# A hybrid decoder layer on eight cores: two x tiles of the third token group loaded from another point and into other slots, and another planned order

## What is computed

```python
h = rmsnorm(x, norm_mix_pre)
q, k, v, u = split(h @ w_in)                 # 512 channels each
q, k = rope(q), rope(k)                      # 8 heads of 64
y_attn = moba_attention(q, k, v)             # each query: own 256-key block (causal)
                                             # and its top 3 earlier blocks by q . mean(k)
y_pool = pool_mixer(u, w_pool, b_pool, pool_scale)   # trailing means over 2/4/8/16 tokens
x = x + rmsnorm(concat(y_attn, y_pool) @ w_out, norm_mix_post)
h = rmsnorm(x, norm_ffn_pre)
f = (silu(conv3(h @ w_gate)) * conv3(h @ w_val)) @ w_down    # 2816 channels each
out = x + rmsnorm(f, norm_ffn_post)
```

## Time and profile before

| | |
|---|---|
| median of 3 runs | 779.73 us (776.73 to 795.33) |
| the profiled execution | 778.17 us |
| its span, slowest core (core 7) | 776.6 us |
| spans of the eight cores | 768.8 to 776.6 us |
| TensorE busy on core 7 | 754.9 us, 97% |
| VectorE, ScalarE, GpSimd busy | 60%, 50%, 37% |

### The profile page before, as it was taken

One profiled execution on the slowest core, in us unless ns is written; L12 is line 12 of the kernel. 1 busy time (PEld: TensorE's weight loads), 2 busy tenths in 40 slices (PEclk: granted clock), 3 DMA queues, 4 the chain that ended last, 5 costly groups with the idle time before them and its releaser, 6 DMA issues.

```text
span 776.6 us, 14872 instructions; the slowest of 8 cores (768.8 to 776.6 us)
## 1 busy us (share of the span) xinstructions
PE 754.9 (97%) x4866; PEld 385.0 (50%) x4866; DVE 469.2 (60%) x702; ACT 387.4 (50%) x619; POOL 286.7 (37%) x309
## 2 busy tenths in 40 slices
PE   7997999999999999999999999999999999999996
PEld 5644655455655555444444444444444444444443
DVE  4786658654555555578787781322877877772223
ACT  3835567158899999554554440211445454441111
POOL 1273324301455560557655562100343444321000
PEclk9899899999999999999999999999999999999998
DMA  8978589119579565678897676342444444001321
GB/s 256 321 243 199 81 187 198 50 28 144 108 193 215 161 170 131 109 136 160 169 194 122 116 115 102 106 166 108 109 82 82 69 71 79 1 0 57 110 99 62
DMA packets 63067, 99.21 MB, mean 128 GB/s; under 512 B 35856, under 2 KB 41872, under 8 KB 61968
## 3 DMA queue, kind: packets, MB, share of 16 engines
q1 hardware_dynamic: 50304, 65.88, 31.2%
q0 software_dynamic: 12688, 32.38, 25.6%
HBM read 100.60 MB, written 16.78 MB: 151 GB/s over the span
## 4 chain that ended last, share of the span: by engine, by line
PE 90%; DMA 3%; DVE 2%; issue 2%; ACT 1%; POOL 1%; SPq 1%; DVEq 0%; ACTq 0%; POOLq 0%
PE ps L954 38%; PE ps L1072 18%; PE ps L830 7%; PE ps L904 7%; PE ps L769 7%; PE ps L674 5%; PE ps L848 4%; DMA MEM<-x 3%; PE ps L1065 1%; PE ps L835 1%; SPq L165 1%; PE ps L797 1%; ACT MEM L844 0%; PE ps L650 0%; DVE MEM L681 0%
## 5 line engine op out<-in xcount | busy, mean ns | idle before, releaser
L954 PE MATMUL ps<-MEM 128*128 128x512 bf16 x1408 | 309.8, 379 | 1.3 <-DVE MEM L975 1.3
L954 PEld LDWEIGHTS ps<-MEM 128*128 128x128 bf16 x1408 | 136.5, 98 | 164.0 <-issue 2.2
L965 ACT ACTIVATE MEM<-ps,MEM 128x1024 f32<-128x1024 f32 x88 | 105.9, 1203 | 147.2 <-PE ps L954 144.0
L844 ACT ACTIVATE MEM<-ps 128x512 bf16<-128x512 f32 (+1 forms) x320 | 149.4, 541 | 38.7 <-PE ps L835 17.1
L991 POOL TENSOR_TENSOR MEM<-MEM 128x1024 bf16<-128x1024 f32 x44 | 105.2, 2391 | 118.9 <-DVE MEM L978 82.0
L968 DVE SCALAR_TENSOR_TENSOR MEM<-ps,MEM 128x1023 f32<-128x1023 f32 x88 | 112.8, 1282 | 57.9 <-ACT MEM L965 57.7
L1072 PE MATMUL ps<-MEM 128*128 128x512 bf16 x660 | 142.8, 379 | 0.0
L971 DVE SCALAR_TENSOR_TENSOR MEM<-ps,MEM 128x1022 f32<-128x1022 f32 x88 | 112.7, 1281 | 8.2 <-DVE MEM L968 0.5
L1072 PEld LDWEIGHTS ps<-MEM 128*128 128x128 bf16 x660 | 64.4, 98 | 78.0
L830 PE MATMUL ps<-MEM 72*128 72x512 bf16 (+1 forms) x320 | 102.8, 349 | 0.1
L604 POOL TENSOR_SCALAR MEM<-MEM 128x1 f32<-128x1 f32 x63 | 13.7, 218 | 197.7 <-ACT MEM L1077 118.8
(11 more groups left out here) (103 smaller groups left out, 620.6 us busy)
## 6 DMA issues: line engine op xcount, KB each, us to landing
MEM<-w_up_r POOLq DMA_DIRECT2D x44, 512.0 KB, 5.5
MEM<-x SPq DMA_DIRECT2D x32, 512.0 KB, 5.5
x1s<-MEM SPq DMA_DIRECT2D x16, 512.0 KB, 5.4
MEM<-x1s SPq DMA_DIRECT2D x16, 512.0 KB, 3.9
out<-MEM SPq DMA_DIRECT2D x15, 512.0 KB, 2.6
MEM<-w_down POOLq DMA_DIRECT2D x22, 256.0 KB, 7.5
MEM<-w_qk SPq DMA_DIRECT2D x4, 1024.0 KB, 20.7
MEM<-MEM SPq DMA_DIRECT2D x24, 128.0 KB, 5.6
```

The source lines that it names most:

```text
L844: op("act", lambda e, c0=c0, u=u, p=p: e.activation(out=PT[p][:, c0:512], in_=bk[u.ids[0]][:, c0:512], func=AF.Exp, scale=SCALE), rd=u.b, ...
L954: mm = op("pe", lambda e, c=c, half=half, pr=pr, ws=ws, tb=tb: e.matmul(bk[pr.ids[tb]], lhsT=wu[ws][:, c, half * 128:(half + 1) * 128], rh ...
L965: op("act", lambda e, pr=pr, ch=ch, ts=ts: e.activation(out=tA[ts], in_=ps(pr)[:, :], func=AF.Identity, scale=cwb[:, ch, 2:3], bias=cwb[:, ...
```

## The change

Six edits. The planner's seed and the size of its jitter change (923 to 1348, 0.15 to 0.3), which reorders the streams. The plan counts 3 us more for the landing of every x load of `load_x`. Tiles 8 to 15 use slot (tt + 2) % 4: tile 8 in xs2, 9 in xs3, 10 in xs0, 11 in xs1. The loads of `next_x` follow that; those of the output projection (`sec1`) keep tt % 4. `bulk` no longer holds the landing of chunk 7, so a load of `next_x` waits for tile 7's landing and for its own slot alone. `scaled` takes the scaling of tile 1 instead of tile 3. All arithmetic, instructions and transfers stay.

```diff
-SEED, SHAKE = 923, 0.15
+SEED, SHAKE = 1348, 0.3
+X_LATE = 3.0
...
-    def dma(self, queue, key, pairs, ..., prio=None, turn=False):
+    def dma(self, queue, key, pairs, ..., prio=None, turn=False, late=0.0):
...
+            fin += o.get("late", 0.0)
             o["t0"], o["t1"] = t, fin
...
-        def load_x(tt, deps=()):
-            s = tt % 4
-            dma("sp", "fx%d" % s, [(xs[s], x_d[tt * 128:(tt + 1) * 128, :])], wr=[buf("xs%d" % s)], deps=deps)
+        def load_x(tt, deps=(), turn=0):
+            s = (tt + turn) % 4
+            dma("sp", "fx%d" % s, [(xs[s], x_d[tt * 128:(tt + 1) * 128, :])], wr=[buf("xs%d" % s)], deps=deps, late=X_LATE)
...
-            xsrc[tt] = (xs[tt % 4], buf("xs%d" % (tt % 4)))
+            xsrc[tt] = (xs[(tt + 2 * (tt > 7)) % 4], buf("xs%d" % ((tt + 2 * (tt > 7)) % 4)))
...
-            if tt == 3:
+            if tt == 1:
                 scaled.append(xb.w[-1])
...
-                load_x(tt, bulk if G < 3 else move1)
+                load_x(tt, bulk if G < 3 else move1, 2)
...
         lw = buf("ws%d" % wslot[7]).w[-1]
-        bulk.append(lw)
```

More of the change, by code:

```diff
@@ L159, in either, with dma @@
         return o
-    def dma(self, queue, key, pairs, rd=(), wr=(), wp=(), deps=(), nbytes=524288, cast=False, prio=None, turn=False):
+    def dma(self, queue, key, pairs, rd=(), wr=(), wp=(), deps=(), nbytes=524288, cast=False, prio=None, turn=False, late=0.0):
         raw = self._collect(queue, rd, wr, wp, deps)
@@ L165, in dma @@
         fn = lambda e: [e.dma_start_transpose(out=o_, in_=i_) if turn else e.dma_start(out=o_, in_=i_) for (o_, i_) in pairs]
-        o = dict(kind="dma", key=key, turn=turn, sig=False, seq=0, slack=0.0, ndma=len(pairs), nbytes=nbytes, cast=cast,
+        o = dict(kind="dma", key=key, turn=turn, sig=False, seq=0, slack=0.0, late=late, ndma=len(pairs), nbytes=nbytes, cast=cast,
                  alts={queue: (fn, (0.62 if queue == "pool" else 0.45) * len(pairs), 0.0)})
```

## The result

| | before | after |
|---|---|---|
| median | 778.78 us | 768.58 us |
| lowest to highest | 776.73 to 795.33 us | 768.33 to 768.68 us |
| span of the slowest core | 776.6 us | 767.1 us (core 1) |
| spans of the eight cores | 768.8 to 776.6 us | 765.8 to 767.1 us |

The changed kernel takes 0.987 of the time before, with a 95% interval of 0.985 to 0.990: 1.3% less, where 1.1% was forecast. In some runs, of every kernel alike, the cores of one die or of both show a lower clock and take longer (the 795.33 here); ratios leave such runs out. Its lines stand one or two further down than those of before (L620 is L622, L674 is L676, L769 is L771, L830 is L832, L848 is L850, L865 is L867).

A forecast was written before the change was run, and what follows sets the result against it. TensorE, busy 754.9 of 776.6 us, was taken as the bound, leaving idle time and low clock to win. 776.6 - 5.2 - 2.0 - 1.3 + 1.3 = 769.4 us of span, 771.0 us as execution time; range 766 to 778.

The forecast's parts named there:

- The stall, -5.2: TensorE's 5.9 us wait at line 848, behind late x loads of tiles 8 and 9, falls to 0.7; bounds 0 and -5.9.
- the clock behind it, -2.0: TensorE's low clock from 78 to 83 us, 2.0 us of work not done, goes if the wait at line 848 goes.
- The start, -1.3: Earlier V casts let 1.9 us of V matmuls fill TensorE's 2.7 us gap; seven tenths last; bounds 0 and -3.6.
- the 1.7 of the upper bound: Clock up from 20.6 to 24 us would win half of those 3.4 us, 1.7; counted at nothing.
- the lower bound's reason: Early V casts might win 0: later weights land no sooner, and TensorE could run dry for them.
- The new order, +1.3: Seed, jitter and 3 us more landing time reorder all streams; taken as 1.3 us lost, twice core 5's 0.7 rounded down.
- The bound of the order: Worst cost of reordering all streams: one more square placed too early, 5.9 + 2.0 us; other bound 0.
- The wait didn't move to the third tile: Rival: VectorE or ScalarE reaches tile 10's squares before its load lands or tile 8 is turned; 773 to 776 us; 0.17.
- the four operations only crowd the engines: Rival: two squares and two scalings, 4.4 us, delay exps and rope products from 60 to 70 us; 775 to 779; 0.08.
- SP held nothing: Rival: SP waits to turn tile 8 ahead of loading tiles 10 and 11; slower, 780 to 783 us; chance 0.07.
- More from the start: Rival: all 3.6 us won there, the stall quite gone, nothing lost to the order; 766.7 us; chance 0.10.
- The rule on packets: DMA engines alternate packets between queue rows, slowing group 0's last q copies; up to 2.7 us more, 772 to 774; 0.03.

The follow-up runs named there:

- the fixed ones: Kernel before with its stream order kept and only named operations moved; with early loads of tiles 8 and 9 alone 773.5 us, ratio 0.993.

## Why the prediction was right

**The stall, -5.2, and the clock behind it, -2.0.** Right: 5.3 of idle time and 2.0 of clock from 62 to 95 us. The early loads alone show the chain of the prediction, and the changed order with late loads shows that the loads are what removes the wait there. But the claim that this wait "goes" by the early load isn't general: the replanned kernel without them has no stall either. The landing of tiles 8 and 9 was forecast by about 59 and came at 56.3 and 59.5 on core 1 (up to 63.6 on core 6). Tiles 10 and 11 landed at 67.4 and 70.2, not at 71 to 73.

**The start, -1.3.** The sum's value holds (1.0 on the pair of cores above, 1.2 at the start of the attention with the casts alone, too little to be told in that kernel's time), but its working doesn't. The gap was to be filled by 1.9 us of matmuls, and the clock was counted at nothing. With the casts alone, busy time from 14 to 24 rose by 0.7 us over the eight cores and not at all on core 7, and most of what was won is clock (0.66 to 1.00 on core 7, 0.72 to 0.86 over the eight). This was the 1.7 of the upper bound, wrongly set to nothing. What takes some back is partly the lower bound's reason, weights that land no sooner: 0.48 us behind q/k weights on core 7 with the casts alone. In the changed kernel TensorE is idle 0.5 to 0.9 us of 24 to 31; on core 1 that wait is for a copy of turned channels (L663), not for weights.

**The new order, +1.3.** The step that failed, in size and sign. On the pair of cores it brought -1.1 (TensorE's waits at line 954, from 300 to 600 us), and against the old order with the same loads and casts it is worth 0.992 to 0.987, some 4 us of device time. The reason is a term that the sum lacks. It took the end of the stall for the end of the matter ("after 95 us TensorE's largest waits are of that size") and did not price the next squares that stand close behind their loads. In the old order with early loads those of group 3 come 3 to 4 us after the issue of loads that then take up to 6.6 us, and TensorE loses 0.6 to 2.0 us to it on cores 3, 4 and 7.

That the time fell into the range is partly luck. Nothing in the sum depends on the seed, so it would have been the same for the kernel with all named edits and the old seed, and that one measured 776.8 us, 0.998. In the old order the sum's loads and casts, without its +1.3, give 768.1 us of span, and the slowest core of that kernel spanned 771.9; in the new order the sum was 2.3 too high. The bound of the order, one more square placed too early at 5.9 + 2.0, was a fair one: the old seed's kernel has squares too early in group 3 and does 5.9 us less work from 95 to 150.

**The rivals.** The wait didn't move to the third tile in the changed kernel; it moved to group 3 in the fixed ones, which is the same mechanism one group on. That the four operations only crowd the engines is refuted: TensorE is busy 32.31 of 33 us from 62 to 95 with all four inside. SP held nothing: tiles 10 and 11 went out at 62.87, ahead of the turning of tile 8 at 69.57. "More from the start" gave the nearest time (766.7), but not by its way, since only 1.0 came from the start.

**The rule on packets.** The last q copies of group 0 were issued at 56.14 and 58.11 on the Pool queue, with rope, x and pooling constants in flight; they took 6.1 and 4.8 us, and the two issued from 51.67 on took 6.2 and 7.0, against 3.1 with free DMA engines in the earlier trace rows. TensorE's longest wait from 53 to 95 us is 0.6, for something else, so this cost nothing; the sum by the rows was the right one. The Trainium skill's page "DMA: Bandwidth & Descriptors", section "Queues, rings and completion order", lets queue rows take turns packet by packet; the longer landings agree with that, though they don't prove that it is the cause.

**What showed it.** Of the signs, all came: two loads at 48.56; no square of group 2 that waits for x; line 850's wait at most 0.5; clock 1.00 from 62 to 80; the first V cast at 12.71 and V matmul at 13.61; cores within 1.3 us; no wait of TensorE over 1 us after 95; and between 24 and 40 us only 0.5 us lost on core 1 (0.7 to 1.5 on the others, where some waits are for casts). The timeline figures are of core 1; the other cores' loads and first casts come within 1.3 us of these.

**What stays open.** Which property of the good orders makes them good beyond the squares of groups 2 and 3 wasn't isolated: the waits at line 954 are gone in the changed kernel, but also without its 3 us and with the old seed, and they are there with the 3 us alone, so no single one of these edits explains them. Why the first load of group 3 takes longer on the cores that issue it last isn't known. Nor can the shares of these three be added, since each replanned kernel is a new draw.

## What to carry to other kernels

When a stall in an in-order stream goes, look at once at the next reader of a load behind it, and at how far it stands behind that load's issue: 3 us were enough while the load took 4.1 us and not when it took 6.6. Here the slowest core still spanned 770.6 us with the first stall gone, and the cores without the second 767.3. A stalled reader can be cured by an earlier load or by a later place in its stream, but a later place must take along the whole chain that hangs on it. Where a planner writes the order, a single edit can't be judged by replanning: hold the order fixed and move only what the edit concerns, and count on about 1% between two seeds.

## What the runs showed of the hardware

The landing time of a 512 KB load of x says as much about the traffic as about its size: 10.3 to 14.7 us before; 7.7 and 10.5 us, then 4.6 and 7.0 us on core 1 of the changed kernel, and 13.0 and 15.4 us for the first two on its core 6, all for the same four loads.

Two idle times of nearly the same length had different prices. TensorE was idle 1.65 us near 105 us on core 4 of the early loads alone and stayed at 1.00 after it. It was idle 2.0 us near 69 us in the changed order with late loads, and its clock was 0.50 from 72 to 74 and 0.76 from 74 to 76. After 3.87 us in the kernel with the later squares it was 0.50 from 110 to 115. So in the first place the idle time was the whole price, and in the second some 1.7 us of work came on top (1.0 in 72 to 74, 0.5 in 74 to 76, 0.2 before). Other work stands around the two, so this pair doesn't settle what decides. The length of the idle time alone doesn't. With the squares later, TensorE of all eight cores stands idle for 3.87 us at the same place; seven then ran at 0.50, and core 3 stayed at 1.00. Core 3, timeline and stretch, then the same stretch of core 0:

```profile
110.37 1.89 PE L739 MATMUL ps<-MEM 128*128 128x512 bf16 x8 [3.87 <-DVE MEM L746]
...
110.00:115.00 5.00, 4.63 (x38) 2.51 (x39) 5.00 (x11) 1.96 (x4) 3.10 (x3) 1.00 0.96 160
...
110.00:115.00 5.00, 4.75 (x26) 2.27 (x27) 4.18 (x9) 0.00 (x0) 3.21 (x3) 0.50 0.99 190
```

Core 3 spans 772.6 us and the others 774.1 to 775.3. In the changed order with late loads, likewise, core 2 was idle 2.75 us and stayed at 1.00, where core 7 fell after 2.0.

In the waits read here VectorE and ScalarE did not pass a waiting instruction. On core 7 of the kernel without the 3 us, ScalarE stood idle for 3.58 us ahead of a square (L621) until 106.64; an exp whose q-times-k matmuls had ended at 104.93 ran only behind it, at 107.69, and TensorE waited 2.62 us for it. The Trainium skill's page "PSUM — Partial Sum Buffer", section "Engine vs sequencer instructions", calls the queues of these engines strict FIFO, and the traces agree.
